# The first recurrence head's first three units begun and weighed inside the differential attention, in the first layer too

## The reference

```python
def step(state, inp):                       # one chunk of 64 tokens of one head
    qi, ki, vi, gi = inp
    bcum = jnp.cumsum(gi, axis=2)
    o_inter = jnp.einsum('bhtk,bhkv->bhtv', qi * jnp.exp(bcum), state)
    rel = bcum[:, :, :, None, :] - bcum[:, :, None, :, :]
    decay = jnp.exp(jnp.where(incl, rel, -jnp.inf))
    scores = jnp.einsum('bhtk,bhsk,bhtsk->bhts', qi, ki, decay)
    o_intra = jnp.einsum('bhts,bhsv->bhtv', scores, vi)
    ...

def diff_softmax_attend(q, keys, vals, lam):
    s = jnp.einsum('bqhmd,bkhmd->bhmqk', q, keys) * (DA_QK ** -0.5)
    p = jax.nn.softmax(s, axis=-1)
    w = p[:, :, 0] - lam * p[:, :, 1]
    return jnp.einsum('bhqk,bkhv->bqhv', w, vals)
```

## Time and profile before

| | |
|---|---|
| median of 3 runs | 3276.86 us (3275.61 to 3285.12) |
| the profiled execution | 3276.41 us, of which the trace spans 3275.1 |
| TensorE busy | 2976.9 us (91%), mean granted clock 0.953 |
| VectorE busy | 1594.6 us (49%) |
| ScalarE busy | 1011.8 us (31%) |
| GpSimd busy | 205.8 us (6%) |
| the first layer's differential attention | from 1119.7 to the fence at 1336.3 us |
| the first layer's recurrence after it | to about 1645 us |

### The profile page before, as it was taken

One profiled execution on the slowest core, in us unless ns is written; L12 is line 12 of the kernel. 1 busy time (PEld: TensorE's weight loads), 2 busy tenths in 40 slices (PEclk: granted clock), 3 DMA queues, 4 the chain that ended last, 5 costly groups with the idle time before them and its releaser, 6 DMA issues.

```text
span 3275.1 us, 44163 instructions
## 1 busy us (share of the span) xinstructions
PE 2976.9 (91%) x18450; PEld 2397.6 (73%) x18450; DVE 1594.6 (49%) x3361; ACT 1011.8 (31%) x1950; POOL 205.8 (6%) x270
## 2 busy tenths in 40 slices
PE   7988899999999998888699999999899797799998
PEld 4657688889977566777558888888666686578886
DVE  3122444444446255676854424334825666645354
ACT  2011432223243155333243211211426344232222
POOL 0000000000000100100000000000211245100001
PEclk9999999999999999799899999999999798899999
DMA  5423231222222110222522121121111010222321
GB/s 181 147 101 126 87 117 47 58 59 59 78 97 103 52 33 1 81 76 79 171 78 90 44 73 65 52 78 65 39 50 28 17 39 14 91 90 85 108 88 67
DMA packets 227299, 246.61 MB, mean 75 GB/s; under 512 B 5553, under 2 KB 193053, under 8 KB 225565
## 3 DMA queue, kind: packets, MB, share of 16 engines
q1 hardware_dynamic: 227100, 243.79, 23.1%
HBM read 234.34 MB, written 9.44 MB: 74 GB/s over the span
## 4 chain that ended last, share of the span: by engine, by line
PE 55%; DVE 10%; ACT 3%; issue 2%; DMA 1%; POOL 0%; ACTq 0%; DVEq 0%; POOLq 0%
PE PS L2054 51%; PE PS L2058 2%; PE PS L2263 1%; ACT AR L174 1%; DVE AR L2777 1%; DVE AR L2792 1%; DVE AR L3032 1%; ACT L169 1%; DVE AR L2776 1%; DVE STAT L2968 1%; DVE AR L2788 1%; DVE AR L2801 0%; DVE EX L3019 0%; ACT EX L174 0%; DMA WR<-in_w_in 0%
## 5 line engine op out<-in xcount | busy, mean ns | idle before, releaser
L2054 PE MATMUL PS<-HI,WC 128*128 128x512 f32 (+2 forms) x1600 | 429.2, 354 | 0.6 <-DVE WC L3013 0.6
L2054 PE MATMUL PS<-AR 128*64 128x64 f32 (+8 forms) x3756 | 314.7, 266 | 63.6 <-ACT AR L174 23.4
L2054 PE MATMUL PS<-WR,HT 128*128 128x256 f32 (+2 forms) x1744 | 362.6, 365 | 10.2 <-ACT AR L174 5.4
L2054 PE MATMUL PS<-HT,WR 128*128 128x256 f32 (+3 forms) x1136 | 351.5, 463 | 20.8 <-ACT EX L174 5.7
L2054 PE MATMUL PS<-DW,DH 128*128 128x384 f32 (+1 forms) x1344 | 357.0, 348 | 0.9 <-DVE AR L2638 0.9
L174 ACT ACTIVATE AR<-PS 128x256 f32<-128x256 f32 (+3 forms) x389 | 165.6, 452 | 616.2 <-PE PS L2054 472.4
L2054 PEld LDWEIGHTS PS<-AR 128*64 128x64 f32 (+5 forms) x3756 | 270.6, 170 | 115.5 <-issue 42.0
L2054 PEld LDWEIGHTS PS<-WR,HT 128*128 128x128 f32 x1744 | 280.5, 198 | 76.4 <-issue 42.7
L2054 PEld LDWEIGHTS PS<-HI,WC 128*128 128x128 f32 x1600 | 284.9, 190 | 42.4 <-DVE WC L3013 1.1
L2054 PEld LDWEIGHTS PS<-HT,WR 128*128 128x128 f32 (+2 forms) x1136 | 211.0, 191 | 129.5 <-issue 90.0
L2054 PE MATMUL PS<-LO,WC 128*128 128x512 f32 (+2 forms) x800 | 282.8, 354 | 0.0
(11 more groups left out here) (354 smaller groups left out, 4419.3 us busy)
## 6 DMA issues: line engine op xcount, KB each, us to landing
WR<-in_w_ffn_in SPq DMA_DIRECT2D x40, 1024.0 KB, 7.5
WR<-in_w_in_b SPq DMA_DIRECT2D x51, 512.0 KB, 6.0
WR<-in_w_mod SPq DMA_DIRECT2D x12, 2048.0 KB, 8.0
WR<-in_w_mod SPq DMA_DIRECT2D x24, 1024.0 KB, 5.4
WR<-in_w_ffn_out SPq DMA_DIRECT2D x22, 1024.0 KB, 4.9
WR<-in_w_in SPq DMA_DIRECT2D x40, 512.0 KB, 4.1
WR<-in_w_out SPq DMA_DIRECT2D x8, 2048.0 KB, 9.4
WR<-in_w_in_a SPq DMA_DIRECT2D x8, 1024.0 KB, 5.3
```

The source lines that it names most:

```text
L2054: mm = lambda o, l, r, start, stop: e.o.matmul(o, l, r, start=start, stop=stop, skip_group_check=True)
```

## The change

In the first layer `levels_early` now takes three units, as in the second: units 0, 1 and 2 are begun and weighed as steps of the filling, four steps instead of two. The begin of unit 1 after the fence is gone, and `recur` finds units 1 and 2 weighed and 2 begun. The rate of the filling for the latent tiles goes from 0.69 to 0.72.

```diff
-        RATE, FILL, MODS = ((1, 2, 2, 1), (1.4, 2.5, 2.5, 1)), ((0.45, 0.69), (0, 0.92)), (1.4, 1.4, 2.2, 2.6)
+        RATE, FILL, MODS = ((1, 2, 2, 1), (1.4, 2.5, 2.5, 1)), ((0.45, 0.72), (0, 0.92)), (1.4, 1.4, 2.2, 2.6)
...
-            first = itertools.chain(prepare(heads[0]), levels_early(heads[0], 1 if both else 3))
+            first = itertools.chain(prepare(heads[0]), levels_early(heads[0], 3))
...
             levels_multiply(heads[0], 0)
-            if both:
-                levels_begin(heads[0], 1)
```

## The result

The changed kernel took 3286.63 us (median of 13 runs, 3282.63 to 3294.88), the kernel before 3276.27 us in the same job (13 runs). The ratio is 1.0032, with an interval of 1.0023 to 1.0041: slower by 10.4 us, just over the 0.3% that the prediction named as its bound of no change. One execution of a later run, e7's, took 4379.02 us in a slow state (granted clock 0.642) and is left out of e7's ratio. The profiled execution took 3284.7 us with a span of 3283.4 us, against 3276.41 and 3275.1 before. In the changed kernel the lines of the helpers stand two lower: the score products are L2261, all other products L2052, the transposes L2056, a begin L2774 and L2775, a weighing L2790, the copy that frees the transposes' bank L2982.

What follows compares the result with a forecast made beforehand. The prediction took the attention's last 55 us to be bound by a round-trip chain through PE, DVE and ACT. +8.6 - 2.9 - 2.6 = +3.1 us gave 3280.0 us, range 3277 to 3284 (0.66).

Steps and rivals of the forecast that it cites:

- its bound of no change: Whole kernel: about 0.3%, 9.8 us, is what a measurement can tell from no change; slower than that had 0.07.
- The tail (+8.6): Last attention turns before the fence: units 1 and 2 begun and weighed there add 8.6 us, bounds +5 and +13.
- Its further mark: Turns 21 and 22: more than 27 us together would decide for DVE as their bound.
- the prediction's laying-out: Turns 8 to 25 laid out on paper from trace durations; longer gaps bring PE's half clock one turn earlier.
- The faster pace (-2.9): Attention turns before 21: filling at 0.72 moves projections earlier, so turn 21 starts 2.9 us sooner; bounds 0 and -4.
- The term's bound of 0: Faster pace in the attention: no gain if PE is full wherever the moved step goes.
- After the fence (-2.6): Behind the fence: unit 1 is already weighed, PE then waits for modulation weights; 2.6 us gained, bounds -0.7 and -4.5.
- the sign: Fence to head 2's projection: 10 to 11 us instead of 13.5, with PE standing before the modulation.
- The rival that the work hides: Attention tail: idle DVE absorbs the added work, about 3274 us; chance 0.25, shared with a larger gain after the fence.
- The rival slower beyond measurement: Turns 21 and 22: DVE becomes their bound, +12.3 us, 3289 us; chance 0.07.
- term 2: Faster pace in the attention: -2.9 us forecast; 0 in the slower rival.
- term 1: Longer attention tail: +8.6 us forecast; +13 in the slower rival.

Runs made afterwards that it cites:

- e7: Kernel before with e6's single places for the units and the first modulation load ahead of the fence; run twice, ratios 1.0002 and 0.9998 to before.
- e1: Kernel before with only the pace raised from 0.69 to 0.72, one unit early as before; 3279.54 us against 3275.81, ratio 1.0010.
- e2: Changed kernel with the old pace 0.69, so three units early alone; 3283.83 us, ratio 1.0026 to before.
- e8: Changed kernel with the pace 0.73 in place of 0.72; ratio 1.0033 to before.
- e11: e9 with the pace 0.67 in place of 0.69; 3282.44 us against 3276.9 for the kernel before, ratio 1.0020.
- e6: Kernel before with the three units' begins and weighings placed singly in turns 16 to 19; ratio 1.0011 to before.
- e4: Kernel before, pace 0.69, with all three units begun and weighed beside the second half's last projections; ratio 1.0018 to before.
- e5: Changed kernel with the first modulation weights loaded in turn 23, ahead of the fence; 3279.58 us, ratio 1.0010 to before.
- e9: Kernel before with only the first modulation weights' load moved ahead of the fence; ratio 0.9998 to before.
- e3: Changed kernel with the modulation's first products three steps later, behind a projection, their load issued as before; 3294.49 us (4 runs), ratio 1.0055 to before.
- e12: e4 with the first modulation weights' load ahead of the fence; 3272.45 us against 3275.44 for the kernel before, ratio 0.9996.

## Why the prediction came out as it did

The predicted 3280.0 us missed the median of 3286.63 by 6.6 us; the time lies inside the range, at its upper end. The forecast of a slower kernel was right, its size was a third of the measured one. Against 3276.41 us the profile has +11.8 us in the two stretches, and the whole +8.3 us in that execution; its first scores had come 1.7 us sooner (1118.04 in place of 1119.72), and the rest gave back 1.8. By the steps:

- **The tail (+8.6) was right, with one part under-sized.** Turn 21 +5.4 us (4.5 expected) and turn 22 +4.0 (4.1), the end 19.37 in place of 19.36: +9.4. PE waits over 3 us for DVE in each, as the prediction said. Its further mark, that the two take more than 27 us together if DVE becomes their bound, was not reached: 25.9, though DVE is busy 15.50 of turn 22's 15.60 us. The 5.4 us of turn 21 are the 3.35 us of state updates and begin(0) in front of the copy (3.45 expected) and 2.0 us of products at half clock (1.0 expected). The half clock had not waited for the longer gaps, as the prediction's laying-out has it: the scores of turn 21 already take 2.93 us in place of 1.56, behind a wait of only 1.04 us, and the maximum that reads them starts 1.37 us later for it. One qualification comes from e1 and e2: turn 21's rise is there with the pace alone (10.26 us in e1), since the faster pace puts begin(0) in front of that turn's copy. Units 1 and 2 are what makes turn 22 15.60 us in place of e1's 7.54. The granted clock of the last 55 us before the fence fell from 0.75 to 0.58; the rule of the Trainium skill that the prediction named against the change (TensorE: Matmul & The Clock Gate, section "Why this matters for your kernels": gaps between bursts of products lose the full clock) agrees with the trace in its direction.
- **The faster pace (-2.9) had the wrong sign; this is the step that failed.** Turn 21 starts 183.2 us behind the first scores in place of 180.8: +2.4. The half that was read from distances held: turn 20 lost 2.0 us (7.14 to 5.13), and the projection moved from turn 16 to turn 12 cost as much as it saved (turns 12 to 16 +1.1, turns 9 to 11 -1.1). The words "is taken up in turns 18 and 19, where PE partly waits for activations" failed. Turn 18, 16.1 us before and to stay at 16 (the expectation of e1), took 21.99 (turns 17 and 18 together +4.7), because the third projection did not fill the wait for the gates' batch but stood behind it. e1 shows it alone, e8 shows that it goes with the batch, and e11 that a projection taken away from these two turns gives back only 0.8 us of its 3.67. What I had not done was to read turn 18 of the kernel before as a turn that already holds two projections around a 6.4 us block of ACT (7.8 in the kernel after). The term's bound of 0 was wrong for the same reason: it let a full PE cost nothing, but not more.
- **After the fence (-2.6) was the right mechanism with a term mis-sized.** PE stands before the modulation while its weights land, as expected, 3.41 us. But it gave 0.0 and not -2.6. The load was issued 1.3 us behind the fence as before, and the modulation's products came 9.8 us behind it in place of 11.7, 1.9 us sooner (2.3 expected). They took 1.89 us as before, where I had hoped for 0.9 less, and the projection took 1.9 us longer (9.13 in place of 7.23), a loss that stood only in the bound, there as 1.6. 1.9 - 1.9 = 0. From the fence to the projection it was 11.6 us, where 10 to 11 had been named as the sign. The other profiles with the same wait have 17.5 to 19.1 us behind the fence (e8, e6, e2, e4), at a clock that is full again sooner, in place of 20.6: so 0 to 3.1 us are gained, by where the clock stands. As e8 has the same queues behind the fence as the kernel after, the 0.0 belongs to this one profile, and part of the miss is the chance of the clock's moment.
- **The rival that the work hides** is refuted by the runs: at three kinds of place the units cost 7.5 (e2), 6.0 (e6) and 3.8 us (e4), and in the kernel after DVE was idle for over 100 us of the attention (228.4 - 124.8). **The rival slower beyond measurement** gave the size nearly, +12.3 us and 3289, but by another route: its term 2 was 0 and its term 1 13, where the run had +2.4 and +9.4.

What e5 and e9 add is that the change was made against one of two causes. Behind the fence PE waited for DVE's weighing and, with that gone, for a DMA that ends only 1.9 us sooner. Only with both taken away does the early work return 6.4 us, and even then it does not pay for the 7.5 us that it costs where the change puts it.

What stays open: what e3 loses behind the first recurrence, and why the clock falls at one moment in one kernel and some us later in another with the same queues (turn 22's scores take 2.40 us in e4 and 1.56 in e12).

## What to carry to other kernels

An engine that is idle half the time still has no free slot if every piece of work stands in the one queue that a round trip passes through. Price an insertion by the instruction behind it and by who waits for that one, and look for a place beside long work on the bound engine. When a pace is changed, list for the old and the new pace which filler stands beside each long block of the other engines; moving one filler saved 2.0 us where it left and cost 4.7 where it went. Count the slow products behind a wait, too: in e6 they made a turn without any wait 3.3 us longer. Before removing a wait, look what arrives next at the same point, and remove both together or neither.

## What the hardware showed

- The same 16 products of a projection took 3.67 us at full clock and 5.30 to 6.18 us behind waits of 3.7 to 5.0 us; 32 products took 7.17 us at full clock and 9.13 us behind the 3.41 us wait, 8.26 us behind one of 4.07 (e2). In these rows a wait was thus worth itself and 1.1 to 2.5 us more of slow products. In e6 and e8, though, the 32 products took 7.17 us behind waits of 3.68 and 3.61 us.
- Up to turn 1, kernels with the same queues differed by 2.9 us (7.39 to 7.48 or 4.5 us) by whether that turn's projection ran at half clock. So two single profiles can differ by some 3 us where the code is the same, and a change of this size needs the runs' medians beside them.
- Three ACT table loads of 1.28 us in one batch took as long together (3.84 us) as the activations between them (3.89 us).
